# Modulation vectors beside the feed-forward products: which layer's tiles are read in which stage, and by which queue

## The chip, the cores and the metric

One core of a Trainium2 chip runs the whole program. The metric is device time in microseconds (us), the median of three runs. The kernel uses TensorE (PE: matmuls), VectorE (DVE), ScalarE (ACT), GpSimd (POOL) and SyncE (SP), which does nothing here but issue DMAs.

## The reference

Two blocks on 512 tokens of width 1024, float32. The first is one hybrid attention layer with a feed-forward (1024 to 4096, squared relu, back to 1024). The second has two layers in which a condition vector and a second, context one modulate every norm and residual; in layer 0 the 256 context tokens go along (768 columns), in layer 1 only the 512 tokens. What the change touches:

```
def modulation(cvec, w_mod, b_mod):          # w_mod[l]: 1024 x 6144
    m = (silu(cvec) @ w_mod + b_mod)         # six vectors of 1024: sh1, sc1, g1, sh2, sc2, g2
for l in range(2):
    sh1, sc1, g1, sh2, sc2, g2 = modulation(c, w_mod[l], b_mod[l])
    csh1, csc1, cg1, csh2, csc2, cg2 = modulation(c_ctx, w_mod[l], b_mod[l])
    hx = rms_norm(x, norm1_g[l]) * (1 + sc1) + sh1
    hc = rms_norm(xc, norm1_g[l]) * (1 + csc1) + csh1     # layer 1: only keys and values of the context
    x = x + g1 * heads_out(...)
    x = x + g2 * (square(relu((rms_norm(x) * (1 + sc2) + sh2) @ w_mlp1[l])) @ w_mlp2[l])
    # context rows the same in layer 0, with cg1, csh2, csc2, cg2
```

So layer 0 needs all 48 columns of 128 for both vectors, layer 1 needs 48 for the condition and 16 (csh1, csc1) for the context.

## The kernel before, in words

Activations lie in SBUF with features on partitions, X[128, 8, 768]. Every float32 weight tile (128 x 1024, 512 KB) is brought by SyncE into `weight_ring` (RING = 5 places), cast by ScalarE into the high half of `weight_split` (4 places, line 2074) and reduced to its low half by VectorE (two tiles of three, L1250) or GpSimd (one of three, L2618). Each product is three matmuls: high by high, high by low, low by high.

A feed-forward runs in 8 groups. A group has four "up" tiles f (24 matmuls of 512 columns each, L590) and then, for the group before, eight "down" tiles m taken in four pairs (24 matmuls a pair, L860). Up tile and down pair are the steps of this text, eight a group, 64 in all. The first two up tiles are computed together, k by k, as the norm delivers. Each engine has its own program with the same loop. At a step it first does `stage(...)`, which casts or splits the weight tile two loads ahead (AHEAD = 2). Then in an up step ScalarE does relu and the squared high part, GpSimd squares once more (L2788) and VectorE makes the low part (L1616); in a down step VectorE adds the two products to the residual (L1631, or L1633 with a gate). At the end of a step the loop calls `next(work)`, and once more after every second down pair, so that a group has ten slots for other work.

That other work is the modulation. A column tile of `w_mod`, transposed, is 128 x 1024: VectorE multiplies it with the condition, broadcast on all partitions, and sums along the row into one column of `MOD` (a dot, L1341 for full rows, L1361 for halves of 512).

- Beside the first block's feed-forward (512 columns): layer 0's 48 tiles and the first 16 of layer 1, two dots a tile (condition and context), a tile a slot. GpSimd fetches them into a ring of two (L2635), tile n + 1 when the last dot of tile n - 1 is done. After them the context rows are loaded and squared.
- Beside layer 0's feed-forward of the second block (768 columns): tiles 16 to 47 of layer 1 in halves, both halves of a tile in turn, one dot each with the condition, a half a slot. GpSimd fetches them into a ring of three that lies in the squares buffer (L2652).

The engines run their queues in order: an engine that waits for a semaphore holds all that is behind it. SyncE's `fill(upto)` (L2934) issues the weight loads in order; load i waits for the low part of load i - 5.

Of the kernel before, what the change touches and what calls it, by code (L numbers as in the profile page):

```python
# [9 lines left out]
F32 = mybir.dt.float32  # L10
# [5 lines left out]
P = 128  # L16
# [187 lines left out]
def build(nc, dr, out_t, plan, known):  # L204
    with ExitStack() as top:
# [64 lines left out]
        mod_ring = place("mod_ring", [P, 2, D], 77824)  # L270
        cond = place("cond", [P, 2, D], 86016)
# [28 lines left out]
        late_cond = place("late_cond", [P, D], 104448)  # L300
        late_half = place("late_half", [P, 32], 108544)
        late_ring = SQ[:, :, :].rearrange("p a t -> p (a t)").rearrange("p (n c) -> p n c", c=512)
# [38 lines left out]
        mod_sem = [led.sem("mod_ring_0"), led.sem("mod_ring_1")]  # L341
# [23 lines left out]
        MOD_TILES = [(0, t) for t in range(48)] + [(1, t) for t in range(16)]  # L365
        MOD_LATE = [(t, half) for t in range(16, 48) for half in range(2)]
# [870 lines left out]
        def vector_program(ve):  # L1237
# [92 lines left out]
            def modulation():  # L1330

                yield
                for n, (l, t) in enumerate(MOD_TILES):
                    yield
                    ve.wait_ge(mod_sem[n % 2], 16 * (n // 2 + 1))
                    if n == 0:
                        ve.wait_ge(mod_cond, 32)
                    for v in range(2):
                        if n + v:
                            ve.wait_ge(*when("mod_vec", ("dot", n - 1, 1) if v == 0 else ("dot", n, 0)))  # L1340
                        ve.tensor_tensor_reduce(out=mod_scratch[:, :], in0=mod_ring[:, n % 2, :], in1=cond[:, v, :], scale=1.0, scalar=0.0, op0=ALU.mult,  # L1341
                                                op1=ALU.add, accum_out=MOD[:, l, v, t:t + 1]).then_inc(*did("mod_vec", ("dot", n, v)))
                    if t == (47, 15)[l]:
                        b0 = VEC[f"bmod_{l}"][0]
                        ve.wait_ge(*when("mod_vec", ("dot", n, 1)))
                        for v in range(2):
                            ve.tensor_tensor(MOD[:, l, v, 0:t + 1], MOD[:, l, v, 0:t + 1], vecs[:, b0:b0 + t + 1], ALU.add).then_inc(*did("mod_vec", ("bias", l, v)))
                            ve.wait_ge(*when("mod_vec", ("bias", l, v)))
                            for w in range(2 if l == 0 else 1):
                                gains(l, v, w)  # L1350

            def late_modulation():

                yield
                ve.wait_ge(late_cond_sem, 16)
                for n, (t, half) in enumerate(MOD_LATE):
                    yield
# [1712 lines left out]
```

## Time and profile before

| | us |
|---|---|
| runs (median, lowest, highest) | 2601.88, 2598.74, 2602.18 |
| the profiled execution, its own time | 2606.4 |
| its span | 2604.6 |
| TensorE matmuls busy | 2426.6 (93%) |
| VectorE busy | 1336.3 (51%) |
| ScalarE busy | 873.2 (34%) |
| GpSimd busy | 621.9 (24%) |

The profile is of one execution. Its times are from the start of the span. Busy is the sum of instructions on an engine; DMA issues, semaphores and branches do not count. A group of instructions shows its busy time, the mean of one in ns, and the idle time of its engine just before it with what ended that idle time. The granted clock is TensorE's, 1.00 for full speed.

### The profile page before, as it was taken

To read this page: it belongs to the slowest core of one execution; us is meant where nothing else is said; L and a number is where in the kernel's file an instruction comes from. 1 tells how busy PE (TensorE), PEld (TensorE's weight loads), DVE (VectorE), ACT (ScalarE), POOL (GpSimd) and SP (SyncE) were. 2 spreads that over 40 slices of the span, in tenths; PEclk is the share of its full clock that TensorE was granted. 3 is DMA by queue.
4 is the path that set the end of the run, shared out by engine and by line. 5 is a ranking of instruction groups with operands and counts; after the bars stand their busy time and mean duration, and the time that the engine had idled before them with its cause. 6 is when DMAs were issued, how large, how long until landed. Compare 5 with 4: busy or idle time off the path is not lost.

```text
span 2604.6 us, 28508 instructions
## 1 busy us (share of the span) xinstructions
PE 2426.6 (93%) x10982; PEld 1812.7 (70%) x10982; DVE 1336.3 (51%) x2107; ACT 873.2 (34%) x1433; POOL 621.9 (24%) x562
## 2 busy tenths in 40 slices
PE   6999889999897997998999999999899999999998
PEld 4665567777676874444888888888676446788886
DVE  4466446878866436344354444444645544443434
ACT  4244433222233212455242222222421564422222
POOL 2533114233321213001042222221122001322221
PEclk9999899999997999998999999999999999899998
DMA  5411124655631221000223333331122011232331
GB/s 187 145 45 41 53 65 166 196 191 188 196 118 40 92 73 55 17 26 17 65 83 104 101 105 99 104 102 61 49 93 79 27 41 57 73 105 82 98 94 51
DMA packets 71075, 233.51 MB, mean 90 GB/s; under 512 B 8911, under 2 KB 12112, under 8 KB 70940
## 3 DMA queue, kind: packets, MB, share of 16 engines
q1 hardware_dynamic: 49328, 165.04, 19.9%
q0 software_dynamic: 18288, 63.49, 7.7%
q10 hardware_dynamic: 3324, 3.14, 0.4%
q8 instruction: 89, 1.46, 0.2%
q14 instruction: 46, 0.38, 0.0%
HBM read 223.73 MB, written 7.90 MB: 89 GB/s over the span
## 4 chain that ended last, share of the span: by engine, by line
PE 76%; DVE 12%; issue 5%; POOL 4%; ACT 3%; DMA 1%; ACTq 0%; DVEq 0%; POOLq 0%
PE psum L590 33%; PE psum L860 19%; DVE mod_scratch L1341 5%; PE psum L1187 4%; PE psum L629 4%; PE psum L1158 3%; PE psum L649 2%; PE psum L1115 1%; PE psum L1173 1%; PE psum L766 1%; POOL hidden_tmp L2788 1%; PE psum L737 1%; POOL weight_split L2618 1%; DVE residual L1631 1%; PE psum L561 1%
## 5 line engine op out<-in xcount | busy, mean ns | idle before, releaser
L590 PE MATMUL psum<-mix_split,weight_split 128*128 128x512 f32 x3792 | 791.1, 369 | 20.4 <-POOL weight_split L2618 6.7
L590 PEld LDWEIGHTS psum<-mix_split,weight_split 128*128 128x128 f32 x3792 | 652.8, 190 | 159.6 <-issue 18.1
L860 PE MATMUL psum<-hidden,weight_split 128*128 128x512 f32 (+1 forms) x3072 | 635.4, 367 | 14.0 <-POOL weight_split L2618 7.7
L860 PEld LDWEIGHTS psum<-hidden,weight_split 128*128 128x128 f32 x3072 | 522.9, 188 | 123.2 <-POOL weight_split L2618 10.9
L2074 ACT CAST weight_split<-weight_ring 128x1024 fp32r<-128x1024 f32 x269 | 276.6, 1040 | 290.0 <-PE psum L860 289.8
L2618 POOL TENSOR_TENSOR weight_split<-weight_ring,weight_split 128x1024 fp32r<-128x1024 f32 x89 | 224.3, 2520 | 409.7 <-ACT weight_split L2074 409.1
L1616 DVE TENSOR_TENSOR hidden<-hidden_tmp,hidden 128x512 fp32r<-128x512 f32 (+1 forms) x128 | 138.1, 1099 | 356.8 <-POOL hidden_tmp L2788 356.8
L1250 DVE TENSOR_TENSOR weight_split<-weight_ring,weight_split 128x1024 fp32r<-128x1024 f32 x180 | 227.2, 1264 | 49.4 <-ACT weight_split L2074 45.8
L2315 ACT ACTIVATE hidden_tmp<-psum 128x512 f32<-128x512 f32 (+1 forms) x128 | 69.0, 539 | 538.8 <-PE psum L590 527.5
L590 PE MATMUL psum<-normed_in,weight_split 128*128 128x512 f32 (+1 forms) x1080 | 220.5, 365 | 9.2 <-DVE normed_in L1304 6.9
L1633 DVE SCALAR_TENSOR_TENSOR residual<-psum,modulation,residual 128x512 f32<-128x512 f32 x192 | 120.7, 657 | 191.5 <-PE psum L860 191.5
L2788 POOL TENSOR_TENSOR hidden_tmp<-hidden_tmp 128x512 f32<-128x512 f32 (+1 forms) x128 | 121.6, 959 | 405.0 <-ACT hidden L2319 404.6
L590 PEld LDWEIGHTS psum<-normed_in,weight_split 128*128 128x128 f32 x1080 | 181.7, 196 | 51.3 <-issue 13.8
L1341 DVE CUSTOM_DVE_ANT_0 mod_scratch<-mod_ring,cond 128x1024 f32<-128x1024 f32 x128 | 172.8, 1350 | 7.8 <-DMA mod_ring<-in_w_mod 3.8
L1158 PE MATMUL psum<-k_heads,q_heads 96*128 96x512 f32 (+1 forms) x288 | 112.2, 511 | 28.5 <-ACT mla_prob L2535 24.8
L1158 PEld LDWEIGHTS psum<-k_heads,q_heads 96*128 96x128 f32 x288 | 51.2, 196 | 90.7 <-issue 49.6
L2087 ACT ACTIVATE squares<-residual 128x512 f32<-128x512 f32 (+2 forms) x60 | 39.4, 659 | 197.6 <-DVE residual L1601 84.9
L629 PE MATMUL psum<-normed,weight_split 128*128 128x512 f32 x360 | 98.0, 424 | 0.8 <-ACT q_and_k L2230 0.5
L1187 PE MATMUL psum<-mla_probT,v_heads 128*64 128x512 f32 (+1 forms) x224 | 97.3, 581 | 1.5 <-DVE mla_probT L2000 1.3
L629 PEld LDWEIGHTS psum<-normed,weight_split 128*128 128x128 f32 x360 | 69.8, 201 | 30.4 <-issue 14.5
L2000 DVE COPY mla_probT<-psum 128x256 f32<-128x256 f32 x72 | 30.2, 419 | 114.2 <-PE psum L1173 114.2
L2635 POOL DMA_DIRECT2D mod_ring<-in_w_mod x64 | 35.8, 560 | 206.4 <-DVE modulation L1341 204.3
(302 smaller groups left out, 2386.3 us busy)
## 6 DMA issues: line engine op xcount, KB each, us to landing
weight_ring<-in_w_mlp SPq DMA_DIRECT2D x128, 512.0 KB, 3.6
weight_ring<-in_w_ff SPq DMA_DIRECT2D x64, 512.0 KB, 4.2
mod_ring<-in_w_mod POOLq DMA_DIRECT2D x64, 512.0 KB, 3.9
weight_ring<-in_w_in SPq DMA_DIRECT2D x45, 512.0 KB, 3.7
squares<-in_w_mod POOLq DMA_DIRECT2D x64, 256.0 KB, 3.1
weight_ring<-in_w_out SPq DMA_DIRECT2D x24, 512.0 KB, 3.6
weight_ring<-in_tables SPq DMA_DIRECT2D x13, 512.0 KB, 3.6
weight_ring<-in_w_v SPq DMA_DIRECT2D x8, 512.0 KB, 4.2
```

Of the source, the lines that this page charges most:

```text
L590: m = pe.matmul(psum[:, b + r, 0:hi - lo], w[:, part_w, :], x[:, part_x, k, lo:hi], start=k == 0 and part_w + part_x == 0, stop=k == KT - ...
L629: m = pe.matmul(bank(b), w[:, part_w, :], HS_1[:, part_x, k, :], start=k == 0 and part_w + part_x == 0, stop=k == KT - 1 and part_w == 1)
L860: mm = pe.matmul(psum[:, b + r, 0:hi - lo], w[:, part_w, :], G[:, part_x, f % (2 * GROUP), lo:hi], start=jj == 0 and part_w + part_x == 0, ...
L1158: m = pe.matmul(psum[:, b + off // 512, 0:pw], QH[0:96, h % 3, q:q + P], KH[0:96, h % 3, k0 + off:k0 + off + pw], start=True, stop=True)
L1187: m = pe.matmul(psum[r0:r0 + DH, b, 0:nq * P], VH[:, k0 // P + t, h * DH:(h + 1) * DH], mla_pt[:, u % 2, t, 0:nq * P], start=t == 0, stop= ...
L1250: ve.tensor_tensor(WS[:, k, 1, 0:w], ring_of(i, 0, w), WS[:, k, 0, 0:w].bitcast(F32), ALU.subtract).then_inc(*did("split_lo_vec", j))
L1341: ve.tensor_tensor_reduce(out=mod_scratch[:, :], in0=mod_ring[:, n % 2, :], in1=cond[:, v, :], scale=1.0, scalar=0.0, op0=ALU.mult, op1=AL ...
L1616: ve.tensor_tensor(G[:, 1, k, a:z], act_tmp[:, f % 2, a:z], G[:, 0, k, a:z].bitcast(F32), ALU.subtract).then_inc(*did(tag + "_vec", ("lo", ...
L1633: ve.scalar_tensor_tensor(out=x, in0=ps, scalar=gate(m + i, a), in1=x, op0=ALU.mult, op1=ALU.add).then_inc(*did(tag + "_vec", ("down", g - ...
L2074: ac.copy(WS[:, j % SPLIT_RING, 0, 0:w], ring_of(i, 0, w)).then_inc(*did("split_hi", j))
L2618: po.tensor_tensor(WS[:, k, 1, 0:w], ring_of(i, 0, w), WS[:, k, 0, 0:w].bitcast(F32), ALU.subtract).then_inc(*did("split_lo_pool", j))
L2788: po.tensor_tensor(x, x, x, ALU.mult).then_inc(*did(tag + "_pool", ("square", f, r)))
```

## The change

Layer 1's 48 tiles all go beside layer 0's feed-forward of the second block; beside the first block's only layer 0's 48 stay. The halves are now taken half by half: first columns 0 to 511 of all 48 tiles, then the rest. The first 16 tiles get a second dot with the context vector, into `late_scratch`. The broadcast condition is held for one half at a time, both vectors, and reloaded at the change of half. Each step has one slot, in all programs (the second `next(work)` is gone); a slot of the second block does two halves. GpSimd's programs `modulation` and `late_modulation` are removed. SyncE issues their fetches between its weight loads, at places given by a new function; the first ring has four places instead of two. Everything else is as before.

```diff
-        mod_ring = place("mod_ring", [P, 2, D], 77824)
-        cond = place("cond", [P, 2, D], 86016)
+        cond = place("cond", [P, 2, D], 77824)
+        mod_ring = place("mod_ring", [P, 4, D], 86016)
...
-        MOD_TILES = [(0, t) for t in range(48)] + [(1, t) for t in range(16)]
-        MOD_LATE = [(t, half) for t in range(16, 48) for half in range(2)]
+        MOD_LATE = [(t, half) for half in range(2) for t in range(48)]
...
             def late_modulation():
...
                 for n, (t, half) in enumerate(MOD_LATE):
-                    yield
+                    if n % 2 == 0:
+                        yield
+                    if t == 0:
+                        ve.wait_ge(late_cond_sem, 32 * (half + 1))
                     x = late_ring[:, n % 3, :]
                     ve.wait_ge(late_sem[n % 3], 16 * (n // 3 + 1))
...
+                    for v in (1, 0) if t < 16 else (0,):
+                        column = late_half[:, v, t:t + 1] if half else MOD[:, 1, v, t:t + 1]
...
+                        ve.tensor_tensor_reduce(out=late_scratch[:, :] if v else x, in0=x, in1=late_cond[:, v, :], scale=1.0, scalar=0.0, op0=ALU.mult,
+                                                op1=ALU.add, accum_out=column).then_inc(*did("late_vec", ("context" if v else "dot", n)))
...
                             next(work, None)
-                            if m % 4 == 0:
-                                next(work, None)
...
-            def modulation():
-                def fetch_tile(n):
-                    l, t = MOD_TILES[n]
-                    if n > 1:
-                        po.wait_ge(*when("mod_vec", ("dot", n - 2, 1)))
-                    po.dma_start(mod_ring[:, n % 2, :], dr["w_mod"][l, t]).then_inc(mod_sem[n % 2], 16)
...
+            def mlp_places(w1, w2):
+
+                out = []
+                for g in range(NGROUP + 1):
+                    out += [load_at[w1(g * GROUP + j)] for j in range(GROUP)] if g < NGROUP else []
+                    out += [load_at[w2(g - 1, m)] for m in range(KT // 2)] if g > 0 else []
+                return out
...
+            fill(load_at["w_ff1", 2])
+            sy.wait_ge(*when("n2_vec", ("scaled", KT - 1, 0)))
+            for v in range(2):
+                sy.dma_start(cond[:, v, :], COND[v:v + 1, :].broadcast_to([P, D])).then_inc(mod_cond, 16)
+            places = mlp_places(lambda f: ("w_ff1", f), lambda g, m: ("w_ff2", (g, m)))
+            for n in range(48):
+                fill(places[max(n - 2, 0)] + RING)
+                if n > 3:
+                    sy.wait_ge(*when("mod_vec", ("dot", n - 4, 1)))
+                sy.dma_start(mod_ring[:, n % 4, :], dr["w_mod"][0, n]).then_inc(mod_sem[n % 4], 16)
+            places = mlp_places(lambda f: ("w_mlp1", (0, f)), lambda g, m: ("w_mlp2", (0, g, m)))
+            fill(places[0] + AHEAD)
+            sy.wait_ge(*when("l0n2_vec", ("lo", KT - 2, 1)))
+            sy.wait_ge(*when("l0n2_pool", ("lo", KT - 1, 1)))
+            for n, (t, half) in enumerate(MOD_LATE):
+                if n % 2 == 0:
+                    fill(places[n // 2 + 1] + RING)
+                if t == 0:
+                    if half:
+                        sy.wait_ge(*when("late_vec", ("dot", n - 1)))
+                    for v in range(2):
+                        sy.dma_start(late_cond[:, v, :], COND[v:v + 1, 512 * half:512 * half + 512].broadcast_to([P, 512])).then_inc(late_cond_sem, 16)
+                if n > 2:
+                    sy.wait_ge(*when("late_vec", ("dot", n - 3)))
+                sy.dma_start(late_ring[:, n % 3, :], dr["w_mod"][1, t][:, 512 * half:512 * half + 512]).then_inc(late_sem[n % 3], 16)
```

## Rows read from the trace of the kernel before

**Rows 1.** The page's busy line of the whole span, by engine
```profile
PE 2426.6 (93%) x10982; PEld 1812.7 (70%) x10982; DVE 1336.3 (51%) x2107; ACT 873.2 (34%) x1433; POOL 621.9 (24%) x562
```

**Rows 2.** TensorE in order of time, first block's feed-forward: start, us, what
```profile
387.87 30.74 PE L590 MATMUL psum<-mix_split,weight_split 128*128 128x512 f32 x120 [2.31 <-DVE mix_split L1302]
...
436.54 17.07 PE L860 MATMUL psum<-hidden,weight_split 128*128 128x512 f32 x72 [0.71 <-POOL weight_split L2618]
...
734.62 44.96 PE L860 MATMUL psum<-hidden,weight_split 128*128 128x512 f32 x192
```

**Rows 3.** TensorE in order of time, layer 1's feed-forward: start, us, what
```profile
2227.49 47.63 PE L590 MATMUL psum<-mix_split,weight_split 128*128 128x512 f32 x192 [2.47 <-DVE mix_split L1304]
2274.96 22.56 PE L860 MATMUL psum<-hidden,weight_split 128*128 128x512 f32 x96
...
2543.76 44.96 PE L860 MATMUL psum<-hidden,weight_split 128*128 128x512 f32 x192
```

**Rows 4.** Groups from 436 to 735 us: busy, mean ns, idle before, releaser
```profile
L1341 DVE CUSTOM_DVE_ANT_0 mod_scratch<-mod_ring,cond 128x1024 f32<-128x1024 f32 x120 | 163.0, 1358 | 5.3 <-DMA mod_ring<-in_w_mod 1.5
L860 PE MATMUL psum<-hidden,weight_split 128*128 128x512 f32 x578 | 140.8, 400 | 14.0 <-POOL weight_split L2618 7.7 <-DVE residual L1631 6.0
L590 PE MATMUL psum<-mix_split,weight_split 128*128 128x512 f32 x576 | 139.0, 400 | 7.2 <-POOL weight_split L2618 6.7 <-DVE weight_split L1250 0.6
...
L2618 POOL TENSOR_TENSOR weight_split<-weight_ring,weight_split 128x1024 fp32r<-128x1024 f32 x17 | 41.0, 2415 | 0.4 <-ACT weight_split L2074 0.2
L1250 DVE TENSOR_TENSOR weight_split<-weight_ring,weight_split 128x1024 fp32r<-128x1024 f32 x33 | 40.3, 1220 | 0.0
L2635 POOL DMA_DIRECT2D mod_ring<-in_w_mod x58 | 32.4, 558 | 190.3 <-DVE modulation L1341 188.2 <-DVE modulation L1347 2.1
L1631 DVE TENSOR_TENSOR residual<-psum,residual 128x512 f32<-128x512 f32 x48 | 30.8, 682 | 0.0
L2788 POOL TENSOR_TENSOR hidden_tmp<-hidden_tmp 128x512 f32<-128x512 f32 x25 | 28.1, 1124 | 6.3 <-ACT hidden L2319 6.1
L1616 DVE TENSOR_TENSOR hidden<-hidden_tmp,hidden 128x512 fp32r<-128x512 f32 x25 | 17.3, 692 | 49.9 <-POOL hidden_tmp L2788 49.9
```

**Rows 5.** The chain that ended last, in order of time: start, us, what
```profile
523.87 1.22 DVE mod_scratch L1341
525.13 1.22 DVE mod_scratch L1341
527.27 2.40 POOL weight_split L2618
...
531.32 1.22 DVE mod_scratch L1341
```

**Rows 6.** Busy time by engine in three stretches; after the engines the granted clock
```profile
605.00:610.00 5.00, 5.00 (x17) 3.91 (x16) 4.96 (x8) 0.00 (x0) 0.57 (x1) 0.66 0.72 224
715.00:720.00 5.00, 3.83 (x12) 3.07 (x13) 4.58 (x5) 1.38 (x2) 2.31 (x3) 0.76 0.61 192
720.00:725.00 5.00, 5.00 (x21) 4.00 (x20) 4.21 (x6) 1.23 (x2) 0.51 (x1) 0.89 0.62 210
```

**Rows 7.** VectorE and GpSimd in order of time near 509 us
```profile
509.30 3.22 DVE L1341 CUSTOM_DVE_ANT_0 mod_scratch<-mod_ring,cond 128x1024 f32<-128x1024 f32 x1
...
509.02 2.40 POOL L2618 TENSOR_TENSOR weight_split<-weight_ring,weight_split 128x1024 fp32r<-128x1024 f32 x1
```

**Rows 8.** The page's DMA issues: count, size, us to landing
```profile
weight_ring<-in_w_ff SPq DMA_DIRECT2D x64, 512.0 KB, 4.2
mod_ring<-in_w_mod POOLq DMA_DIRECT2D x64, 512.0 KB, 3.9
```

**Rows 9.** ScalarE in order of time near 396 us
```profile
395.97 1.99 ACT L2074 CAST weight_split<-weight_ring 128x1024 fp32r<-128x1024 f32 x2
```

**Rows 10.** Busy time by engine, 1340 to 1847 us (layer 0's feed-forward)
```profile
1340.00:1847.00 507.00, 507.00 (x2898) 442.01 (x2896) 226.71 (x360) 120.30 (x183) 129.02 (x139) 1.00 0.30 95
```

**Rows 11.** Groups from 1400 to 1780 us, the dots of layer 1's modulation
```profile
L1361 DVE CUSTOM_DVE_ANT_0 squares<-squares,late_cond 128x512 f32<-128x512 f32 x55 | 36.7, 682 | 0.0
```

More of the change, by code:

```diff
@@ L340, in build @@
         ring_sem = [led.sem(f"ring_{i}") for i in range(RING)]
-        mod_sem = [led.sem("mod_ring_0"), led.sem("mod_ring_1")]
+        mod_sem = [led.sem(f"mod_ring_{i}") for i in range(4)]
         late_sem = [led.sem(f"late_ring_{i}") for i in range(3)]
@@ L1340, in modulation @@
                             ve.wait_ge(*when("mod_vec", ("dot", n - 1, 1) if v == 0 else ("dot", n, 0)))
[L1341 to L1350, printed above, removed]
+                        ve.tensor_tensor_reduce(out=mod_scratch[:, :], in0=mod_ring[:, n % 4, :], in1=cond[:, v, :], scale=1.0, scalar=0.0, op0=ALU.mult,
+                                                op1=ALU.add, accum_out=MOD[:, 0, v, n:n + 1]).then_inc(*did("mod_vec", ("dot", n, v)))
@@ L1352, in late_modulation @@
+                b0 = VEC["bmod_0"][0]
+                ve.wait_ge(*when("mod_vec", ("dot", 47, 1)))
+                for v in range(2):
+                    ve.tensor_tensor(MOD[:, 0, v, :], MOD[:, 0, v, :], vecs[:, b0:b0 + 48], ALU.add).then_inc(*did("mod_vec", ("bias", v)))
+                    ve.wait_ge(*when("mod_vec", ("bias", v)))
+                    for w in range(2):
+                        gains(0, v, w)
             def late_modulation():
                 yield
-                ve.wait_ge(late_cond_sem, 16)
@@ L1369, in late_modulation @@
-                gains(1, 0, 1)
+                for v, z in ((0, 48), (1, 16)):
+                    m = MOD[:, 1, v, 0:z]
+                    ve.tensor_tensor(m, m, late_half[:, v, 0:z], ALU.add).then_inc(*did("late_vec", ("whole", v)))
+                    ve.wait_ge(*when("late_vec", ("whole", v)))
+                    ve.tensor_tensor(m, m, vecs[:, b0:b0 + z], ALU.add).then_inc(*did("late_vec", ("bias", v)))
+                    ve.wait_ge(*when("late_vec", ("bias", v)))
+                    for w in range(2 - v):
+                        gains(1, v, w)
@@ L2331, in mlp @@
                             next(work, None)
-                            if m % 4 == 0:
-                                next(work, None)
                 for _ in work:
@@ L2337, in beside_mlp @@
             def beside_mlp():
-                for _ in range(1 + len(MOD_TILES)):
+                for _ in range(1 + 48):
                     yield
@@ L2788, in mlp @@
                                     po.tensor_tensor(x, x, x, ALU.mult).then_inc(*did(tag + "_pool", ("square", f, r)))
-                            for f in fs:
-                                next(work, None)
                     if g > 0:
@@ L2793, in mlp @@
                             stage(*w2(g - 1, m // 2))
-                            next(work, None)
-                            if m % 4 == 0:
-                                next(work, None)
-                for _ in work:
-                    pass
             def filters(l):
@@ L2897, in block_1 @@
                 normed_split("n2", HS_T1, X1, None)
[L2899 removed]
+                mlp("mlp1", lambda f: ("w_ff1", f), lambda g, m: ("w_ff2", (g, m)), act_tmp_1, X1)
             def block_2(l):
```

57 lines of the change are left out of this document (13 added, 44 removed).

## The prediction

> **What bounds the kernel now.** I read the page's engine line first: TensorE's matmuls are busy 93% of the span [rows 1], so only time in which TensorE stands still or runs at a lower clock can be won. Next I followed TensorE alone in order of time through the three feed-forward stages. The first block's (512 columns) starts at 387.87 and ends at 734.62 + 44.96 = 779.58: 391.7 us [rows 2]. The last one (layer 1's, same shape, nothing beside it) starts at 2227.49 and ends at 2588.72: 361.2 us, without a gap in its timeline [rows 3]. The difference, 30.5 us, is what the modulation now costs, and it is my ceiling. The rows by group must be seen as follows. From the first "down" product at 436.54 to the last at 734.62 there are 6 groups of 8 steps: 298.1 / 6 = 49.7 us a group; in the last stage (2543.76 - 2274.96) / 6 = 44.8, 5.6 a step [rows 2, 3]. That is 4.9 lost per group, 29.4 in six.
>
> What is late? In those six groups TensorE waits 14.0 + 7.2 us, mostly for GpSimd's split of a weight tile, then for VectorE's residual [rows 4]. GpSimd is not busy: its line of 58 DMA issues has 190.3 us of waiting ahead of it, 188.2 of that for VectorE's dot products [rows 4]. So the fetch of tile n + 1, which must wait until dot n - 1 has emptied its half of the ring of two, holds GpSimd's splits and squares behind it. The chain shows one turn: dot, GpSimd split, GpSimd square, next dot: from 523.87 to 531.32, 7.45 us for a step that TensorE does in 5.6 [rows 5]. VectorE's four groups of work add up to 163.0 + 40.3 + 30.8 + 17.3 = 251 of 299 us [rows 4]: nearly full, but not the wall alone; the loop through GpSimd is. A second loss follows: after two of the stalls the granted clock is 0.66, 0.76 and 0.89 in 5 us stretches [rows 6] (1.00 is 2.4 GHz, so they are means with the 1.2 GHz level in them), which is 5 x (0.34 + 0.24 + 0.11) = 3.5 us. The 21.2 us of waits and these 3.5 leave 5.8 of the 30.5 for restarts at some twenty gaps.
>
> **The change part by part.**
>
> *Taken from the first stage.* 16 of 64 tiles, 32 dots, go; the slots go from ten a group to eight, one a step, so the double slots after every second "down" pair vanish. Per group VectorE loses 4 dots of 1.224 plus its gap; dots stand 1.26 apart [rows 5]: 5.0 us.
>
> *GpSimd's fetches go.* 64 issues of 0.558 (35.7 us) and the wait behind which split and square stood [rows 4]. This is the main term. What is late next is VectorE or the pair of both, so I sum a group anew. Dots 16 x 1.26 = 20.2; splits 16/3 x 1.220 = 6.5; residuals 8 x 0.682 = 5.5; low parts 4 x 0.692 = 2.8: 35.0 for VectorE. GpSimd: splits 8/3 x 2.415 = 6.4; squares 4 x 1.04 (they run 1.01 to 1.12 [rows 4, 5]) = 4.2: 10.6. TensorE needs 44.8. If both run side by side the bound is 44.8 (stall 0); if never, 45.6 (stall 0.8 a group). Why never? VectorE's dot that starts 0.28 us after a GpSimd split took 3.22 instead of 1.224 [rows 7]: it stood still until the split was over. And the same sum for before, 10 tiles, is 40.0 + 10.6 = 50.6 against 49.7 measured, so "almost never together" fits. The residual reads PSUM and its mean is unstretched, so some overlap is left: I take 0.4 us a group, 3 us in the stage with what single steps lose, and keep 0 and 10 as ends.
>
> The Trainium skill (SBUF — State Buffer, "Who interferes with whom") says that a VectorE instruction with two SBUF inputs and a GpSimd instruction that reads SBUF exclude each other for the whole instruction. The stretched dot agrees. By it the freed GpSimd collides with dots more often; it is the rule that speaks against a full gain, and by it the sum is the 45.6 above or worse.
>
> *SyncE's queue.* It now has 50 more issues in the first stage and 100 in the second, between weight loads. SyncE computes nothing. What is queued behind a tile's wait is the next weight load: load n + 4 goes out after tile n, whose wait is dot n - 4, made by VectorE in step n - 2. VectorE ends that step about 3.2 us after TensorE has (residual 0.68, two dots). From there to TensorE's step n + 4 are five steps, 28 - 3.2 = 24.8 us. The way is 4.2 to land [rows 8], a cast of 1.0 [rows 9], a split of at most 2.4, and up to 5 behind dots in the queue: 13. So 12 us of slack; cost 0. Tile n itself is issued after step n - 2 and read in step n + 2: 3 steps, 16.8 us, against 3.9 to land [rows 8]. Cost 0.
>
> *Start of the stage.* The fourth weight tile used to lie in the ring; ScalarE casts the third and fourth together at 395.97 [rows 9]. Now it leaves only after the norm's last scaling, behind the two broadcasts of the condition: three 512 KB transfers, so I estimate 4.2 to 8 us later, landing 400 to 404, cast and split by 407. TensorE comes to it at 436.54 - 0.71 - 5 x 5.6 = 407.8 [rows 2]. ScalarE's relu of the first two tiles waits behind that cast, with free banks for two more tiles. 0 to 2 us; I take 0.
>
> *Put into the second stage* (layer 0's feed-forward, 768 columns). TensorE is busy 507.0 of 507 us there and VectorE 226.7 (45%) [rows 10]. Before there are 64 dots of 0.682 [rows 11]; after 96 + 32 = 128. The 64 more are 64 x 0.76 (0.08 a dot is my estimate for the gap, from 1.26 against 1.224 and a read of the sum) = 49 us of VectorE in about 48 steps of 8.4 (= 5.6 x 768/512). In the 16 steps that also have context dots, four dots are 3.0, a split 1.2, the residuals of two tiles 2.1 (2 x 0.682 x 1.5 for the width): 6.3, or 7.5 with a GpSimd split in place of VectorE's. Under 8.4; cost 0, bound 16 x 1 us if everything blocks. Fetches: each half tile is issued when dot n - 3 is done, a step or more ahead (8.4 against 3.9 for a whole tile). The reload of the condition between halves delays one step's dots by at most 5 us, where splits are made two steps ahead: 0. GpSimd loses 64 issues here too, with no stall of TensorE to give back.
>
> *Tail.* The context rows and their squares move from the last two groups to the one before; VectorE's tail is bound by the residual-square chain. 0.
>
> **Sum.** 30.5 - 3 = 27.5 saved, rounded to 27. The profiled execution took 2606.4 us and would take 2579; it stands 4.5 above the median of the three runs, 2601.88, so the median after is 2575.
>
> **The rivals.**
>
> *A, the forecast*: stage at 362 to 368 us; 2571 to 2581. For it: the last stage's 361.2 without gaps, and a VectorE sum under 44.8. Against it: little room. Chance 0.72.
>
> *B, the stall is only halved*: freed splits and squares collide with dots. Then a group is 45.6 plus what VectorE still idles for the square; it idles 49.9 us ahead of 25 low parts, 2.0 each, of which the square itself is 1.04 [rows 4]. Half of the rest, 4 x 1 / 2 = 2, gives 47.6; 2.8 x 6 = 17 us kept: 2601.9 - 30.5 + 17 = 2588, and 2582 to 2595 as its span. For it the stretched dot, against it that the same addition would put before at over 52. Chance 0.18. The rule that I cited from the Trainium skill (SBUF — State Buffer, "Who interferes with whom") describes this mechanism; the trace agrees, with the dot of 3.22 us.
>
> *C, nothing comes*: the dots alone, not GpSimd's wait, set the pace and the clock or a ring takes back the 5.0 a group; within 0.2% (5.2 us). Against it: two thirds of TensorE's waits (14.4 of 21.2) name GpSimd. Chance 0.03.
>
> *D, slower*: weight loads starve behind a tile's wait in SyncE's queue. Place: the load behind dot n - 4, or in the second stage dot n - 3. It decides from where the 12 us of slack are used up, that is when VectorE runs over two steps behind; then each turn of dot, landing 4.2, cast 1.0, split 2.4 lies on the path. At 1 us a step in both stages' 96 steps that is +96 less the 30 saved: about 2665; below 0.3 us a step it would still be no loss. Against it: SyncE's slack is five steps, and VectorE catches up in each up-phase. Chance 0.07.
>
> **How the numbers follow.** Predicted is A's 2575. A measurement tells about 0.2% (5.2 us) from no change; the three runs lie 3.4 apart. The range 2569 to 2587 holds A with the full ceiling of 30.5 and the runs' spread below, the 10 us end of the start and lock costs, and nearly half of B. Faster 0.90 (A and B), same 0.03, slower 0.07.
>
> **What the profile after would show.** Right: no GpSimd DMA issues in either stage, groups of 44.8 to 45.4 us, TensorE idle in the stage under 4 us, clock 1.00 throughout, the layer-0 stage still without a gap. GpSimd's splits start right after ScalarE's cast. B: TensorE waits for VectorE's splits or residuals, and dots of over 3 us appear many times. D: SyncE's waits name the modulation line and casts wait for weight DMAs. What would make me wrong: a gap at the start of either stage for the fourth weight tile, a clock that falls without a stall, or context steps over 8.4 us.

## The result, and the profile after

Four runs of the changed kernel took 2569.32 us in the median (2566.28 to 2570.05), four of the kernel before on the same chip 2602.03: a ratio of 0.9872 (0.9855 to 0.9889). That is 32.7 us less, where I forecast 27. On a second chip the ratio was 0.9858 (0.9844 to 0.9871).

The page's busy line after [rows 1]:

```profile
PE 2414.5 (94%) x10982; PEld 1808.9 (70%) x10982; DVE 1372.1 (53%) x2171; ACT 872.9 (34%) x1433; POOL 566.5 (22%) x431
```

GpSimd has 131 instructions fewer: its 128 fetches and the three broadcasts of the condition. GpSimd's count and busy time do hold these issues (L2635 in [rows 4] is a group of its own, 558 ns each), so part of the 55.4 us by which its busy time fell is issuing. VectorE has 64 instructions more, which are 32 dots more in all (32 fewer beside the first block, 64 more halves beside layer 0), because each dot is followed by a short instruction that reads its sum.

TensorE in order of time through the first block's feed-forward [rows 2]: start, us, what.

```profile
390.24 47.43 PE L590 MATMUL psum<-mix_split,weight_split 128*128 128x512 f32 x192 [2.31 <-DVE mix_split L1302]
437.52 22.56 PE L860 MATMUL psum<-hidden,weight_split 128*128 128x512 f32 x96
459.92 22.56 PE L590 MATMUL psum<-mix_split,weight_split 128*128 128x512 f32 x96
...
706.32 44.96 PE L860 MATMUL psum<-hidden,weight_split 128*128 128x512 f32 x192
756.51 1.83 PE L548 MATMUL psum<-c_ones,squares 128*128 128x1 f32 x8 [5.24 <-DVE squares L1261]
```

From 390.24, the first row's start, to 706.32 + 44.96 = 751.28 TensorE waits nowhere (the 2.31 in the first row lies before it). The stage takes 361.0 us, against 391.7, as long as layer 1's [rows 3], and a group (706.32 - 437.52) / 6 = 44.8. The last row is the start of the next norm, 5.24 us behind; before it was 6.73.

The groups from 438 to 706 us, the same six feed-forward groups as [rows 4]: busy, mean ns, idle before, releaser.

```profile
L860 PE MATMUL psum<-hidden,weight_split 128*128 128x512 f32 x575 | 135.1, 395 | 0.0
L1341 DVE CUSTOM_DVE_ANT_0 mod_scratch<-mod_ring,cond 128x1024 f32<-128x1024 f32 x87 | 121.8, 1400 | 1.5
...
L2082 ACT CAST weight_split<-weight_ring 128x1024 fp32r<-128x1024 f32 x48 | 49.4, 1042 | 75.3 <-DMA weight_ring<-in_w_ff 61.4 <-PE psum L860 14.0
L2624 POOL TENSOR_TENSOR weight_split<-weight_ring,weight_split 128x1024 fp32r<-128x1024 f32 x16 | 43.2, 2699 | 55.4 <-ACT weight_split L2082 55.4
...
L1626 DVE TENSOR_TENSOR hidden<-hidden_tmp,hidden 128x512 fp32r<-128x512 f32 x24 | 31.9, 1328 | 44.0 <-POOL hidden_tmp L2757 44.0
```

Two things are new beside the empty wait of TensorE. ScalarE's casts now wait 61.4 us for weight loads, where they had waited for none. And VectorE is slower for each instruction: dots 1400 ns in the mean (1358 before), low parts 1328 (692 before). Unstretched they are 1.224 and 0.692 [rows 4, 5], so the stretch (mean less unstretched, times the count) was 120 x 0.134 = 16 us in six groups before, and is 87 x 0.176 + 24 x 0.636 = 15.3 + 15.3 = 31 now. That is what rival B said: a freed GpSimd stands in VectorE's way. It costs TensorE nothing here: VectorE still idles 44.0 us ahead of the low parts. One stretched dot in both engines' order of time [rows 7], and the end of the stage:

```profile
542.20 3.30 DVE L1341 CUSTOM_DVE_ANT_0 mod_scratch<-mod_ring,cond 128x1024 f32<-128x1024 f32 x1
541.16 3.26 POOL L2624 TENSOR_TENSOR weight_split<-weight_ring,weight_split 128x1024 fp32r<-128x1024 f32 x1 [9.03 <-ACT weight_split L2082]
...
751.88 1.90 DVE L1261 TENSOR_TENSOR squares<-squares 128x512 f32<-128x512 f32 x1 [0.69 <-ACT squares L2095]
750.88 2.35 POOL L2624 TENSOR_TENSOR weight_split<-weight_ring,weight_split 128x1024 fp32r<-128x1024 f32 x1 [22.65 <-ACT weight_split L2082]
```

Layer 0's feed-forward with its 128 dots, busy time by engine and the granted clock [rows 10]; then its dots from 1400 to 1780 us [rows 11]; then ScalarE's cast of the fourth weight tile [rows 9]:

```profile
1275.14:1815.00 539.86, 539.86 (x3072) 470.52 (x3072) 301.39 (x520) 140.10 (x219) 117.82 (x93) 1.00 0.36 115
```

```profile
L1368 DVE CUSTOM_DVE_ANT_0 late_ring<-late_ring,late_cond 128x512 f32<-128x512 f32 x73 | 58.8, 832 | 0.6
```

```profile
405.27 1.05 ACT L2082 CAST weight_split<-weight_ring 128x1024 fp32r<-128x1024 f32 x1 [5.88 <-DMA weight_ring<-in_w_ff]
```

TensorE is busy for the whole of 539.86 us there. The dots are stretched here too, 832 ns for 682. The fourth tile was cast from 405.27 and split by VectorE until 407.58, where I had allowed 407; TensorE comes to it at 437.52 - 5 x 5.6 = 409.5 and shows no gap.

SyncE's own waits, for the first ring (L2926) and the late one (L2941): us in total, times, longest.

```profile
SPq L2926 <- DVE modulation L1341: 215.1, 44, 14.7
...
SPq L2941 <- DVE modulation L1368: 169.9, 33, 15.3
SPq L2941 <- DVE late_half L1368: 162.3, 33, 12.1
```

So the wait did not vanish; it moved from GpSimd to SyncE, with weight loads queued behind it.

The spans of the two profiled executions differ by 36.4 us, more than the medians. I cut both along TensorE's timeline, and did so for every run below, before taken a second time among them (us):

| kernel | first block's feed-forward | TensorE's wait behind it | layer 0's feed-forward | from the norm behind it to layer 1's | span |
|---|---|---|---|---|---|
| before | 391.7 | 6.7 | 539.8 | 377.2 | 2604.6 |
| before, again | 392.0 | 6.7 | 539.8 | 373.9 | 2602.4 |
| after | 361.0 | 5.2 | 539.9 | 373.6 | 2568.2 |
| after, again | 361.3 | 5.2 | 539.9 | 373.9 | 2568.5 |
| pool_ring2 | 363.1 | 5.2 | 539.8 | 377.2 | 2573.6 |
| pool_ring4 | 361.3 | 5.2 | 539.8 | 377.4 | 2572.4 |
| sync_ring2 | 373.8 | 5.2 | 539.8 | 374.0 | 2582.6 |
| gpsimd_64_ring4 | 370.2 | 6.7 | 539.9 | 373.4 | 2578.5 |
| sync_64 | 373.7 | 6.7 | 539.9 | 373.9 | 2579.8 |
| sync_64_ahead | 374.1 | 6.7 | 539.9 | 374.0 | 2586.4 |
| dots_20 | 374.5 | 5.2 | 539.9 | 373.6 | 2578.9 |
| dots_24 | 399.8 | 5.2 | 539.8 | 377.1 | 2611.0 |
| context_late | 361.1 | 6.7 | 539.4 | 377.2 | 2568.9 |
| tail_gpsimd | 361.1 | 2.5 | 539.9 | 373.5 | 2565.6 |

The change is worth 30.7 us in the stage and 1.5 behind it: 32.2. The stretch from the norm behind layer 0's feed-forward to layer 1's is 377 or 374 us in kernels whose code there is the same; 3.6 of the 36.4 are that, not the change. Two other stretches that the table leaves out, also untouched, move more: the start of the first feed-forward lies between 384.8 and 390.8 us, and from the norm behind it to layer 0's it takes 517.9 to 523.8. So of a span or a median only what the rows locate is given to a change below.

The second chip's medians (2605.33 and 2568.93, the runs called after_again below) lie 36.4 us apart, 33.6 to 40.6 by the interval, more than the 32.2 that I can locate. The spans of the two second profiles differ by 33.9. What the rest is stays open.

### The profile page after: what moved, and what is told of

Same layout as the page of the kernel before. It is cut to its first block, busy times and chain, and to the rows that moved or that the text cites. A ratio compares the mean times of both kernels' runs of the same rounds, so it can differ in the third digit from the quotient of the medians.

```text
span 2568.2 us, 28604 instructions
## 1 busy us (share of the span) xinstructions
PE 2414.5 (94%) x10982; PEld 1808.9 (70%) x10982; DVE 1372.1 (53%) x2171; ACT 872.9 (34%) x1433; POOL 566.5 (22%) x431
## 3 DMA queue, kind: packets, MB, share of 16 engines
q0 software_dynamic: 3520, 11.58, 1.3%
## 4 chain that ended last, share of the span: by engine, by line
PE 87%; DVE 6%; ACT 3%; issue 3%; POOL 1%; ACTq 0%; DVEq 0%; POOLq 0%
PE psum L590 38%; PE psum L860 24%; PE psum L1187 4%; PE psum L629 4%; PE psum L1158 3%; PE psum L649 2%; PE psum L1115 2%; PE psum L1173 1%; PE psum L766 1%; PE psum L737 1%; PE psum L561 1%; PE psum L548 1%; DVE mla_stat L1994 1%; PE psum L784 1%; PE psum L1050 1%
## 5 line engine op out<-in xcount | busy, mean ns | idle before, releaser
L2624 POOL TENSOR_TENSOR weight_split<-weight_ring,weight_split 128x1024 fp32r<-128x1024 f32 x89 | 233.9, 2628 | 544.2 <-ACT weight_split L2082 543.8
L1626 DVE TENSOR_TENSOR hidden<-hidden_tmp,hidden 128x512 fp32r<-128x512 f32 (+1 forms) x128 | 156.2, 1240 | 321.8 <-POOL hidden_tmp L2757 321.8
L2757 POOL TENSOR_TENSOR hidden_tmp<-hidden_tmp 128x512 f32<-128x512 f32 (+1 forms) x128 | 127.9, 1010 | 613.5 <-ACT hidden L2327 613.2
L1341 DVE CUSTOM_DVE_ANT_0 mod_scratch<-mod_ring,cond 128x1024 f32<-128x1024 f32 x96 | 133.5, 1391 | 1.7
L2541 ACT ACTIVATE mla_prob<-psum,mla_stat 128x768 f32<-128x768 f32 (+1 forms) x80 | 65.4, 817 | 40.0 <-DVE mla_stat L1998 22.4
```

Source lines behind the costliest of these rows:

```text
L1626: ve.tensor_tensor(G[:, 1, k, a:z], act_tmp[:, f % 2, a:z], G[:, 0, k, a:z].bitcast(F32), ALU.subtract).then_inc(*did(tag + "_vec", ("lo", ...
L2624: po.tensor_tensor(WS[:, k, 1, 0:w], ring_of(i, 0, w), WS[:, k, 0, 0:w].bitcast(F32), ALU.subtract).then_inc(*did("split_lo_pool", j))
L2757: po.tensor_tensor(x, x, x, ALU.mult).then_inc(*did(tag + "_pool", ("square", f, r)))
```

## Experiments: fewer dots, a deeper ring, another queue

The change does three things to the first stage at once: 20 dots a group become 16, the ring goes from two to four places, and the fetches move from GpSimd to SyncE. Six kernels take them apart. One pair stays together: the dots fell from 20 to 16 along with the double slots, so at a ring of two it is not shown which of the two helped. At a ring of four the slots made little difference: 20 dots a group in eight slots (dots_20 below) give a stage of 374.5, in ten slots (sync_64) 373.7.

**pool_ring2**: the changed kernel with the 48 fetches back on GpSimd, ring of two. Only the number of dots and the slots differ from before.

```diff
-            for n in range(48):
-                fill(places[max(n - 2, 0)] + RING)
-                if n > 3:
-                    sy.wait_ge(*when("mod_vec", ("dot", n - 4, 1)))
-                sy.dma_start(mod_ring[:, n % 4, :], ...)
+                    if n > 1:
+                        po.wait_ge(*when("mod_vec", ("dot", n - 2, 1)))
+                    po.dma_start(mod_ring[:, n % 2, :], ...)     # in GpSimd's modulation(), once a slot
```

> The changed kernel, with the first stage's 48 fetches back on GpSimd and a ring of two; one tile a step, 16 dots a group. Theory Q (the loop through GpSimd's queue set the pace before): a step is dot, fetch wait, split, square, low part, as in the rows of before 7.45 us with a split and 5.17 without; with one tile a step the down steps have no low part in the loop, so most of a group fits: groups of 45 to 46.5 us, TensorE waits for GpSimd's splits come back, stage 363 to 373 us, 2570 to 2581. Theory L (the amount of VectorE's dots set the pace): groups of 44.8, stage 361, 2569 as the changed kernel.

Measured: 2576.5 us, ratio 0.9883 (0.9857 to 0.9909), the stage 363.1. Groups from 437 to 715 us:

```profile
L860 PE MATMUL psum<-hidden,weight_split 128*128 128x512 f32 x615 | 144.9, 395 | 0.2 <-POOL weight_split L2624 0.2
...
L1341 DVE CUSTOM_DVE_ANT_0 mod_scratch<-mod_ring,cond 128x1024 f32<-128x1024 f32 x87 | 120.6, 1386 | 2.3 <-DMA mod_ring<-in_w_mod 0.8
...
L2751 POOL DMA_DIRECT2D mod_ring<-in_w_mod x42 | 23.9, 568 | 150.2 <-DVE modulation L1341 150.2
```

GpSimd still stands 150.2 us behind a tile's wait, and TensorE waits 0.2 (the 2.1 us that the stage lacks to 361.0 lie almost all before 457 us). The loop from dot to split to square to dot exists as before; with four dots a group fewer and no double slots it turns within 5.6 us. A group is 44.9. Theory Q had the loop and its waits in the rows (150.2) but expected groups of 45 to 46.5; the stage is at the edge of its range. 28.6 of the 30.7 us come without touching the queue that I called the main term.

**gpsimd_64_ring4**: the kernel before, 20 dots a group, GpSimd's fetches, but a ring of four.

```diff
-                    if n > 1:
-                        po.wait_ge(*when("mod_vec", ("dot", n - 2, 1)))
-                    po.dma_start(mod_ring[:, n % 2, :], dr["w_mod"][l, t]).then_inc(mod_sem[n % 2], 16)
+                    if n > 3:
+                        po.wait_ge(*when("mod_vec", ("dot", n - 4, 1)))
+                    po.dma_start(mod_ring[:, n % 4, :], dr["w_mod"][l, t]).then_inc(mod_sem[n % 4], 16)
```

> The kernel before with a ring of four in place of two in the first stage; GpSimd still fetches all 64 tiles, 20 dots a group, so its issue waits for dot n - 4 and in effect for nothing. If GpSimd's waiting made the 2.8 us a group between the kernel before (49.7) and the one with SyncE (46.9): 46.9 to 47.5, 2583 to 2588 beside 2606. If it was the issuing itself, 0.56 us a tile on GpSimd: 49 to 49.7, 2600 to 2605.

Measured: 2580.28 us, 0.9904 (0.989 to 0.9919), the stage 370.2. The same view, and a stretch of it by engine:

```profile
L1341 DVE CUSTOM_DVE_ANT_0 mod_scratch<-mod_ring,cond 128x1024 f32<-128x1024 f32 x119 | 173.3, 1456 | 3.8
...
L2635 POOL DMA_DIRECT2D mod_ring<-in_w_mod x57 | 31.8, 558 | 90.2 <-DVE modulation L1341 88.8 <-DVE modulation L1347 1.4
```

```profile
500.00:560.00 60.00, 58.98 (x252) 47.25 (x253) 59.08 (x80) 15.76 (x20) 21.45 (x20) 1.00 0.64 211
```

Two more places alone give 21.5 us, a little more than I expected (a group is 46.3, not 46.9 to 47.5). The wait of GpSimd falls from 188.2 [rows 4] to 88.8, and now VectorE is the wall: 59.08 of 60 us in this stretch. So the loop through GpSimd was the bound, as I read it, but it has two cures, fewer dots or a deeper ring, and they are not additive: 28.6 and 21.5 for a ceiling of 31.

**sync_64**: the kernel before, 64 tiles and ten slots kept, fetched by SyncE with the ring of four.

```diff
+                places += [load_at["w_ff2", (g - 1, m)] for m in (0, 0, 1, 2, 2, 3)] if g > 0 else []
+            for n, (l, t) in enumerate(MOD_TILES):
+                fill(max(places[n + 2] - 4, places[0]) + RING)
+                if n > 3:
+                    sy.wait_ge(*when("mod_vec", ("dot", n - 4, 1)))
+                sy.dma_start(mod_ring[:, n % 4, :], dr["w_mod"][l, t]).then_inc(mod_sem[n % 4], 16)
```

> The kernel before, with only the first stage's 64 fetches moved to SyncE and a ring of four; 20 dots a group in ten slots, the second stage as before. Theory Q: the stage falls to 361 to 365 us, groups 44.8 to 45.4, time 2570 to 2574: all of the gain with no tile moved. Theory L: VectorE 40.0 and GpSimd 10.6 us a group, never together, give 50.6; groups stay at 49 to 50.6 us and the time at 2598 to 2604.

Measured: 2582.91 us, 0.9911 (0.9887 to 0.9936), the stage 373.7, 3.5 more than with GpSimd's fetches at the same depth, and a group 46.9. Both theories missed: Q, which gave the queue the whole gain (361 to 365), and L, which had none of it coming (groups of 49 to 50.6). Groups from 437 to 715 us:

```profile
L590 PE MATMUL psum<-mix_split,weight_split 128*128 128x512 f32 x571 | 137.6, 400 | 8.1 <-DVE weight_split L1250 8.1
...
L2074 ACT CAST weight_split<-weight_ring 128x1024 fp32r<-128x1024 f32 x48 | 50.2, 1046 | 122.4 <-DMA weight_ring<-in_w_ff 122.1 <-issue 0.2
```

The casts wait 122 us for weights. Are these late loads what costs? **sync_64_ahead** lets each load out one step earlier:

```diff
-                fill(max(places[n + 2] - 4, places[0]) + RING)
+                fill(max(places[n + 2] - 3, places[0]) + RING)
```

> The kernel before with 64 fetches on SyncE as in the run with 373.7 us, but each weight load let out one step earlier than there, ahead of the tile. With GpSimd's fetches and the same ring of four the stage was 370.2, with SyncE's ScalarE's casts waited 122 us for weight loads. If that queueing (rival D, in small) made the 3.5 us: stage 369.5 to 371, casts wait under 50 us for loads. If not: 373 to 374.

Measured: 2583.13 us, 0.9924 (0.9907 to 0.994), the stage 374.1. The same group, and a stretch by engine:

```profile
L2074 ACT CAST weight_split<-weight_ring 128x1024 fp32r<-128x1024 f32 x47 | 48.7, 1043 | 94.3 <-DMA weight_ring<-in_w_ff 88.9 <-PE psum L860 5.2 <-issue 0.2
```

```profile
500.00:560.00 60.00, 57.87 (x247) 45.76 (x246) 59.12 (x76) 14.89 (x18) 14.88 (x7) 1.00 0.62 212
```

A quarter of the casts' wait went (122 to 89, where I had reckoned with under 50) and the stage did not move. VectorE is at 59.12 of 60 us. That speaks for VectorE and against the late loads as what sets the time here, but 89 us of the casts' wait are still there, so the test is a partial one. What makes SyncE's version 3.5 us longer than GpSimd's is not settled.

**pool_ring4** and **sync_ring2** fill the table at 16 dots: the changed kernel with the fetches on GpSimd and a ring of four, and with SyncE's fetches and a ring of two.

```diff
 # pool_ring4: as pool_ring2, but
+                    if n > 3:
+                        po.wait_ge(*when("mod_vec", ("dot", n - 4, 1)))
 # sync_ring2
-                if n > 3:
-                    sy.wait_ge(*when("mod_vec", ("dot", n - 4, 1)))
-                sy.dma_start(mod_ring[:, n % 4, :], ...)
+                if n > 1:
+                    sy.wait_ge(*when("mod_vec", ("dot", n - 2, 1)))
+                sy.dma_start(mod_ring[:, n % 2, :], ...)
```

> The changed kernel with the first stage's 48 fetches on GpSimd and a ring of four. If SyncE is not needed once there are 16 dots a group and a ring of four: no gap, stage 361.0 to 361.5, the changed kernel's time. If GpSimd's issues (0.56 us a tile) still cost: about as with the ring of two, 363, 1.5 to 2 us more.

> The changed kernel with SyncE's ring of two. Tile n now waits for dot n - 2 and the weight load behind it goes out two steps later, 11.2 of my 12 us of slack. If rival D's point is where I put it: first gaps, stage 361 to 366, ScalarE's casts wait for weight loads far longer than the 67 us of the changed kernel. If the slack was larger: 361.

Measured: pool_ring4 2569.55 us, 0.9863 (0.9845 to 0.9881), the stage 361.3, the changed kernel's time. sync_ring2 2584.43 us, 0.9925 (0.9909 to 0.994), the stage 373.8. Its groups from 437 to 715 us:

```profile
L860 PE MATMUL psum<-hidden,weight_split 128*128 128x512 f32 x576 | 139.0, 398 | 5.2 <-POOL weight_split L2624 2.9 <-DVE residual L1641 1.6 <-DVE weight_split L1250 0.5
...
L2082 ACT CAST weight_split<-weight_ring 128x1024 fp32r<-128x1024 f32 x49 | 51.5, 1051 | 180.6 <-DMA weight_ring<-in_w_ff 169.6 <-PE psum L860 11.0
L1250 DVE TENSOR_TENSOR weight_split<-weight_ring,weight_split 128x1024 fp32r<-128x1024 f32 x32 | 41.6, 1301 | 19.2 <-ACT weight_split L2082 19.2
```

Here the chain of rival D is whole: casts wait 169.6 us for weight loads that stand in SyncE's queue behind a tile's wait, VectorE's splits wait 19.2 us for the casts (GpSimd's 122.3), and TensorE waits for the splits, most of all GpSimd's. The loss is 12.8 us in the stage, more than the 0 to 5 that I expected. With a ring of two SyncE is the wrong queue (373.8) and GpSimd nearly the right one (363.1); with a ring of four it makes no difference. (By the page's queue lines GpSimd's fetches run in a software queue, which had 18288 packets in before, 10720 in pool_ring4 and 3520 in the changed kernel, and SyncE's in a hardware one; at a ring of four that made no difference to the stage either.) At 16 dots moving the fetches to SyncE bought nothing that the ring alone does not buy.

## Experiments: how much room VectorE has

Before, 20 dots a group, and after, 16, lie on the two sides of a limit. **dots_20** and **dots_24** are the changed kernel with the condition's dot of every second tile, or of every tile, made twice (the second writes the same value): 20 and 24 dots a group, rings and queues as after.

```diff
+                        if v == 0 and n % 2 == 0:        # dots_24: v == 0
+                            ve.tensor_tensor_reduce(out=mod_scratch[:, :], in0=mod_ring[:, n % 4, :], in1=cond[:, 0, :], ...)
```

> The changed kernel with one dot of every second tile of the first stage made twice (the same result written again), 20 dots a group. If VectorE's and GpSimd's work never run together: 40.0 + 10.6 = 50.6 us a group, stage 396, time about 2604. If side by side: 40.0 is under 44.8, stage 361, time 2569. In the trace of the changed kernel half of GpSimd's time stretched a VectorE instruction (5.1 of 10.6 us a group), which gives 40.0 + 5.1 = 45.1: stage 361 to 364, 2569 to 2572.

> The changed kernel with one dot of every tile of the first stage made twice, 24 dots a group. Never together: 30.2 + 14.8 + 10.6 = 55.6 us a group, six groups with dots 65 us over the floor, about 2634. Half together: 45.0 + 5.1 = 50.1, 32 us over, about 2600. Side by side: 45.0, 2570.

Measured: dots_20 2581.03 us, 0.99 (0.9878 to 0.9921), the stage 374.5; dots_24 2610.4 us, 1.002 (1.0007 to 1.0034), the stage 399.8. A group, read from the starts of the "down" products, is 44.8 at 16 dots, 46.75 at 20 and 50.75 at 24. The groups from 437 to 715 us, dots_20 first, and for dots_24 a stretch by engine:

```profile
L860 PE MATMUL psum<-hidden,weight_split 128*128 128x512 f32 x569 | 138.3, 402 | 6.5 <-DVE residual L1645 6.4
...
L1630 DVE TENSOR_TENSOR hidden<-hidden_tmp,hidden 128x512 fp32r<-128x512 f32 x24 | 34.0, 1417 | 15.5 <-POOL hidden_tmp L2761 15.5
```

```profile
L860 PE MATMUL psum<-hidden,weight_split 128*128 128x512 f32 x558 | 141.0, 413 | 17.6 <-DVE weight_split L1250 9.9 <-DVE residual L1645 7.7
...
L1250 DVE TENSOR_TENSOR weight_split<-weight_ring,weight_split 128x1024 fp32r<-128x1024 f32 x29 | 47.0, 1621 | 0.0
```

```profile
500.00:560.00 60.00, 55.14 (x222) 43.26 (x221) 59.38 (x78) 15.01 (x18) 17.25 (x8) 0.94 0.51 169
```

VectorE is full at 24 dots. From 20 to 24 a group grows by 4.0 us, less than the four dots' 5.0; from 16 to 20 by 1.95. Taking 5.0 away for each four dots gives 41.7 from the one and 40.7 from the other, so my estimate for 16 dots is 3 to 4 us a group of room under TensorE's 44.8. It is a rough one, because at 20 dots VectorE is not full: it idles 15.5 us ahead of the low parts, and TensorE waits 6.4 us for residuals all the same. At 24 dots my sums were 45.0 of pure VectorE work (35.0 + 8 x 1.26) and 10.6 of GpSimd's; 50.75 is about the first plus half of the second. "Never together" (55.6) is refuted, "always together" (45.0) too. But "half together" is no rule: for 20 dots it gave 45.1 and a stage of 361 to 364, and 46.75 and 374.5 came. By the means the stretch at 20 dots is (87 x 0.246 + 33 x 0.226 + 24 x 0.725) / 6 = 7.7 us a group (dots, VectorE's splits, low parts), for 5.1 at 16 dots: it grows with VectorE's load, and single steps are late before the sum is.

## Experiments: the tail, and the kernels again

**context_late**: the changed kernel, but the context rows' squares are made two a step and five steps later, so that the last two fall at the start of the last group; before, the last group had some of them too.

```diff
-                for _ in range(3):
+                for _ in range(8):
                     yield
                 for t in range(KT):
                     square_sum("n3c", t, SQ, SQ[:, 1, :], S, T2)
-                    yield
+                    if t % 2:
+                        yield
```

> The changed kernel with the context rows' squares two a step in four steps, the last two in the first step of the last group, as before. If they make the tail's 1.5 us: TensorE's wait at the end of the stage is 6.7 instead of 5.2 us, time 1.5 us more than the changed kernel. If not: 5.2.

Measured: 2576.85 us, 0.9884 (0.9868 to 0.99), its profiled execution 2570.67. TensorE in order of time:

```profile
703.03 44.97 PE L860 MATMUL psum<-hidden,weight_split 128*128 128x512 f32 x192
754.74 1.84 PE L548 MATMUL psum<-c_ones,squares 128*128 128x1 f32 x8 [6.74 <-DVE squares L1261]
```

The gap is 6.74 again, the 6.73 of before; so the 1.5 us of the tail come from where the context's squares lie. VectorE adds the last two in the last group (at 733.85 and 734.75 here, at 765.43 and 766.33 in before, and no later than 729.52 in the changed kernel), between residuals that the next norm waits for. The term that I had put at 0 is 1.5. (The median, 8 us above the changed kernel's on that chip where I expected 1.5, is not explained; the profiled execution is the lowest of the four, and its stage is 361.1.)

**tail_gpsimd**: the tail has a second cost, seen in the rows above at 751.88: a sum of squares that took 1.90 us for 0.69 beside GpSimd's split. Here GpSimd makes the gained squares' sums of the last group, and its last split goes behind them.

```diff
-                                    if gained:
-                                        square_sum(gained, m + i, squares_2, squares_2[:, 1, :], 0, hi)
+                            if m < KT - 2:
+                                stage(*w2(g - 1, m // 2))
+                            for n in (m, m + 1):
+                                if n:
+                                    ...
+                                    po.tensor_tensor(squares_2[:, 0, :], squares_2[:, 0, :], squares_2[:, 1, :], ALU.add)
+                            if m == KT - 2:
+                                stage(*w2(g - 1, m // 2))
```

> The changed kernel with the sums of the squares with gain in the last group on GpSimd, and GpSimd's next weight split behind them. VectorE's pair then costs about 5.0 us instead of 6.7, under TensorE's 5.6, and no square is blocked by a split: TensorE's wait at the end of the stage falls from 5.2 to 2.3 to 3.3 us, time 2 to 3 us under the changed kernel. If GpSimd's sums block VectorE's: 4.5 to 6 us, no gain.

Measured: 2563.5 us, 0.9836 (0.9822 to 0.985), the best of all. VectorE and GpSimd in order of time:

```profile
749.50 0.69 DVE L1261 TENSOR_TENSOR squares<-squares 128x512 f32<-128x512 f32 x1 [0.69 <-ACT squares L2093]
750.31 1.27 POOL L2768 TENSOR_TENSOR squares_with_gain<-squares_with_gain 128x512 f32<-128x512 f32 x1 [0.83 <-ACT squares_with_gain L2093]
751.54 2.34 POOL L2622 TENSOR_TENSOR weight_split<-weight_ring,weight_split 128x1024 fp32r<-128x1024 f32 x1
```

No sum is stretched, and the gap is 2.5 us instead of 5.2: 2.8 shown by the trace. 1.2 of them are the sum that is no longer stretched (1.90 to 0.69); the others come with the fewer sums that VectorE makes in its chain, which this run does not take apart. The medians on that chip differ by 5.4, 2568.93 to 2563.5; where the other 2.6 lie is not shown.

**after_again** and **before_again** are the two kernels unchanged.

> The changed kernel as it is, once more. My ceiling for it was 30.5 us in the stage; the first timing gave 32.7 between the medians and the stretch between the stages is 1.5 us shorter. Theory S (stage 30.5 and tail 1.5, the rest is scatter): 31 to 33.5 us under the kernel before, ratio 0.987 to 0.988, stage at 361.0. Rival C (it also saves clock elsewhere): over 34 us under it.

> The kernel before, once more, for its trace. In four of the traces so far the stretch from the end of layer 0's feed-forward to the start of layer 1's, which the change doesn't touch, took 377.2 us (the kernel before among them), in six 373.4 to 373.9. If that follows from how a run's clock falls and not from the kernel: this trace may show either, stage 391 to 392 in any case. If the kernel before always has the longer one, its trace shows 377 again and the change is worth 3.5 us more there.

Measured: 2568.93 us, 0.9858 (0.9844 to 0.9871), and 2602.8 us, 0.9999 (0.9988 to 1.001). After_again's stage and tail are as first measured, 361.3 and 5.2, but its median is 36.4 us under the kernel before, outside the 31 to 33.5 of theory S; a gain elsewhere, rival C of that expectation, is neither located in a trace nor excluded. Before_again has 373.9 where the first profile of the same kernel had 377.2.

## Where the prediction held, and the steps that failed

**Held: the stage's ceiling and the place.** The stage against layer 1's gave 30.5; 30.7 came. Groups are 44.8, the layer-0 stage has no gap, the clock is 1.00 from 438 to 751 us, the fourth tile cost nothing, and the 64 dots more in the second stage cost nothing though they were stretched to 832 ns (VectorE is busy 301.4 us of 540 there, 55.9 more than before, where I reckoned 49).

**What failed in the sum.** It was 30.5 - 3 = 27.5, with the tail at 0. Both terms are wrong, and both to the same side. On the forecast's base of 2601.88 the ratio 0.9872 gives 2568.6, just under the range's lower end of 2569: that end held the ceiling of the stage (2571.4) and 2.4 of scatter, and nothing outside the stage.

**Failed step: the residual stall, 3 us.** I kept 0.4 us a group; it is 0. I had set the bound as 44.8 or 45.6 by adding all of GpSimd's work to VectorE's. The collisions came, and doubled (16 to 31 us in six groups), but of GpSimd's 10.6 us a group only 31 / 6 = 5.1 fell on VectorE: 35.0 + 5.1 = 40.1, not 45.6. The check that had convinced me (40.0 + 10.6 = 50.6 against 49.7 for before) was a coincidence: before's pace was the loop's, for with the same 20 dots and a ring of four a group is 46.3.

**Failed step: the tail, put at 0.** It is 1.5 (context_late). I had VectorE's chain of residuals and squares as the bound there, and left out that the context's last two sums stand in that chain. These two terms are 4.5 of the 5.7 between 27 and 32.7; my rounding down of 27.5 is 0.5 more. The last 0.7 is inside the interval of the ratio, which is 0.0017 x 2602 = 4.4 us to each side.

**Failed step: the cause given most weight.** I called GpSimd's fetches the main term. Taking 16 tiles out gives 28.6 with the queue as it was (pool_ring2), and the ring alone 21.5 (gpsimd_64_ring4). That the stage came out near the forecast is luck in this respect: both cures lead to the same ceiling, whoever fetches. Had the change moved only the queue, at 20 dots, my argument would have overstated it: sync_64, with the ring of four as well, gives 18.0 in the stage.

**Rival B** had the right mechanism and the wrong price, since VectorE's room absorbed it. The Trainium skill (SBUF — State Buffer, "Who interferes with whom") says that such pairs exclude each other for a whole instruction. The single rows agree (3.30 us beside a split of 3.26), but the rule says nothing of how often two engines meet, and here it was half of GpSimd's time. **Rival D** was rightly put off by slack, but some of my 12 us were used: casts did wait 61.4 us for weight loads, and nothing behind them was late. The slack is also smaller than I reckoned. The ring of two takes 11.2 us of it away, which should have left 0.8, and the stage lost 12.8. (By its own terms D's time was 2571 + 96 = 2667, not 2665.)

## What to carry to other kernels

When a loop of waits across engines sets the pace, look for all its cures (less work in the loop, a deeper ring, another queue) and run each alone: here fewer dots (with the double slots gone) gave nearly all of it, the ring was a substitute, and the queue was worth nothing beside them. A wait that is moved to another engine's queue is as long there (GpSimd's 188 us in six groups, SyncE's 215 over the stage), so choose the queue by what stands behind it and how many steps of slack that has. And when two engines lock each other out, do not add all of one to the other: take the stretch from the mean duration against the undisturbed one, and compare it with the idle time that the engine has left. Take it anew for another load: it was 5.1 us a group at 16 dots and 7.7 at 20.

## What the runs showed of the hardware

Two things I had not expected. Which instructions are stretched depends on who meets whom: in pool_ring4 the dots were stretched and the low parts not (dots 1534 ns, 87 x 0.310 = 27 us in six groups), with SyncE's fetches both (15.3 + 15.3); the total changed by 4 us. The groups from 437 to 715 us of pool_ring4:

```profile
L1341 DVE CUSTOM_DVE_ANT_0 mod_scratch<-mod_ring,cond 128x1024 f32<-128x1024 f32 x87 | 133.5, 1534 | 1.5
...
L1626 DVE TENSOR_TENSOR hidden<-hidden_tmp,hidden 128x512 fp32r<-128x512 f32 x25 | 17.3, 693 | 50.8 <-POOL hidden_tmp L2773 50.8
```

And an untouched stretch has two lengths. Busy time by engine and the granted clock, first after, then pool_ring4, at the same distance behind layer 0's feed-forward to within 0.3 us:

```profile
1860.00:1880.00 20.00, 19.85 (x87) 14.35 (x86) 11.02 (x17) 4.33 (x7) 7.88 (x9) 1.00 0.29 102
1880.00:1900.00 20.00, 17.54 (x82) 14.34 (x81) 8.55 (x10) 7.10 (x10) 5.00 (x5) 0.91 0.49 158
```

```profile
1860.00:1880.00 20.00, 19.86 (x81) 14.38 (x80) 11.35 (x18) 4.13 (x6) 6.46 (x7) 0.92 0.31 103
1880.00:1900.00 20.00, 17.91 (x73) 14.48 (x72) 8.38 (x10) 7.30 (x10) 6.41 (x7) 0.83 0.44 145
```

The same program there, the same busy time of every engine to within 0.4 us over the two stretches, and a granted clock of 1.00 and 0.91 in one, 0.92 and 0.83 in the other. By an estimate that is 20 x (0.08 + 0.08) = 3.2 us, most of the 3.8 by which the whole stretch is longer (377.4 against 373.6). What makes the clock fall in one and not in the other is not shown. Both lengths occur with before (377.2, 373.9), so it belongs to the execution. A difference of a few us between single profiles of this kernel has to be located before it is given to a change.
